# The state-space stage of a two-layer trunk: three spreads, both own products, the output weights and the PE's overflow loops moved

## The reference

```python
u   = rms_norm(x).reshape(b, s, 64 groups, 16)
bu  = einsum('blgc,gpc->blgp', u, bbar)            # complex, 64 states a group
x_k = scan of  x_k = abar * x_{k-1} + bu_k  over the 256 positions
y   = Re(C x_k) + d_skip * u
y   = gelu(y);  a, g = split(y @ w_out);  out = a * sigmoid(g)
```

## Time and profile before

| | us |
|---|---|
| median of three runs | 727.4 |
| lowest, highest | 727.02, 729.13 |
| the profiled execution, in all | 729.73 |
| its span, first to last instruction | 728.0 |
| PE busy in the span | 633.8 |
| DVE, ACT, POOL busy | 192.7, 136.9, 190.2 |
| mean granted TensorE clock | 0.949 |
| DMA, mean over the span | 335 GB/s |

### The profile page before, as it was taken

One profiled execution on the slowest core, in us unless ns is written; L12 is line 12 of the kernel. 1 busy time (PEld: TensorE's weight loads), 2 busy tenths in 40 slices (PEclk: granted clock), 3 DMA queues, 4 the chain that ended last, 5 costly groups with the idle time before them and its releaser, 6 DMA issues.

```text
span 728.0 us, 13207 instructions
## 1 busy us (share of the span) xinstructions
PE 633.8 (87%) x5575; PEld 404.7 (56%) x5575; DVE 192.7 (26%) x499; ACT 136.9 (19%) x301; POOL 190.2 (26%) x226
## 2 busy tenths in 40 slices
PE   8999998999999988999496989999999699596473
PEld 6888886777556646666162655446564366253130
DVE  3234233255231023102012780126302013002003
ACT  3111322232021011020014331004211012010003
POOL 1001120250699997781941000021000000000001
PEclk9999999999998999799799899999999899899898
DMA  9997967555999999999999556965798999999992
GB/s 313 352 296 158 379 172 228 217 198 215 406 421 420 423 419 415 406 425 420 423 381 344 183 160 265 422 273 203 292 423 346 424 421 422 419 421 421 420 396 75
DMA packets 86707, 244.21 MB, mean 335 GB/s; under 512 B 28052, under 2 KB 56948, under 8 KB 62580
## 3 DMA queue, kind: packets, MB, share of 16 engines
q1 hardware_dynamic: 85188, 237.50, 84.7%
q0 software_dynamic: 1056, 5.24, 1.9%
q10 hardware_dynamic: 400, 0.57, 0.3%
HBM read 239.08 MB, written 4.22 MB: 334 GB/s over the span
## 4 chain that ended last, share of the span: by engine, by line
PE 70%; DMA 20%; SPq 3%; issue 2%; DVE 2%; ACT 2%; POOL 0%; DVEq 0%; POOLq 0%
DMA ring<-in_moe_w_down 11%; PE ps L1962 11%; DMA ring<-in_moe_w_up 9%; PE ps L1698 8%; PE ps L2238 8%; PE ps L2002 7%; PE ps L1833 6%; PE ps L2022 4%; PE ps L1701 4%; PE ps L1762 4%; PE ps L1678 3%; PE ps L1829 2%; SPq L467 2%; PE ps L1895 1%; PE ps L1800 1%
## 5 line engine op out<-in xcount | busy, mean ns | idle before, releaser
L1962 PE MATMUL ps<-ring,xg 128*32 128x256 f32 x1904 | 126.3, 405 | 29.2 <-DMA ring<-in_moe_w_gate 15.1
L1962 PEld LDWEIGHTS ps<-ring,xg 128*32 128x32 f32 x1904 | 70.7, 117 | 80.1 <-issue 51.9
L2002 PE MATMUL ps<-ring,hidT 128*32 128x512 f32 x488 | 65.2, 655 | 18.1 <-DMA ring<-in_moe_w_down 14.0
L2022 PE MATMUL ps<-y_sb,pickT 128*128 128x512 f32 x128 | 59.5, 605 | 3.1 <-ACT y_sb L1012 1.6
L1698 PE MATMUL ps<-xnT,ring 128*128 128x256 f32 x256 | 57.8, 382 | 1.1 <-ACT xnT L888 0.8
L845 POOL TENSOR_TENSOR xh<-x,normw 128x1024 f32<-128x1024 f32 x1 | 2.4, 2357 | 213.3 <-DVE x L1413 213.3
L2238 PE MATMUL ps<-ring,yT 128*128 128x512 f32 x128 | 56.3, 595 | 1.6 <-ACT yT L1065 0.9
L1698 PEld LDWEIGHTS ps<-xnT,ring 128*128 128x128 f32 x256 | 47.8, 190 | 9.0 <-issue 1.0
L1418 DVE TENSOR_TENSOR hid<-sg,ps 128x256 f32<-128x256 f32 (+1 forms) x18 | 7.2, 399 | 163.4 <-ACT sg L985 152.2
L2002 PEld LDWEIGHTS ps<-ring,hidT 128*32 128x32 f32 x488 | 16.6, 119 | 51.5 <-issue 44.9
L1833 PE MATMUL ps<-pick,xn 128*128 128x256 f32 x192 | 44.0, 382 | 0.0
(11 more groups left out here) (370 smaller groups left out, 861.2 us busy)
## 6 DMA issues: line engine op xcount, KB each, us to landing
ring<-in_moe_w_up SPq DMA_DIRECT2D x59, 1024.0 KB, 17.3
ring<-in_moe_w_gate SPq DMA_DIRECT2D x59, 1024.0 KB, 12.7
ring<-in_moe_w_down SPq DMA_DIRECT2D x53, 1024.0 KB, 16.8
ring<-in_attn_w_qkv SPq DMA_DIRECT2D x11, 1024.0 KB, 11.8
ring<-in_moe_w_down SPq DMA_DIRECT2D x16, 512.0 KB, 13.2
ring<-in_ssm_w_out SPq DMA_DIRECT2D x8, 1024.0 KB, 12.4
ring<-in_attn_w_o SPq DMA_DIRECT2D x4, 1024.0 KB, 10.5
chunk_inputs<-turned POOLq DMA_DIRECT2D x3, 1024.0 KB, 10.5
```

The costliest lines, as they stand in the source:

```text
L1962: ins = mm(ps[CAP * h:CAP * (h + 1), GUB, F * half:F * (half + 1)], p.xg[:, c, CAP * (ROUND * r + h):CAP * (ROUND * r + h + 1)], w, start= ...
L2002: ins = mm(ps[CAP * h:CAP * (h + 1), DNB + b, :], hidT[:, r, j, CAP * h:CAP * (h + 1)], w, start=(j == 0), stop=(j == FT - 1), tile_positi ...
L2022: ins = mm(ps[:, u, :], p.pickT[rows, r, tt * P:(tt + 1) * P], y_sb[rows, r, 512 * b:512 * (b + 1)], start=(r == 0), stop=(r == p.rounds - 1))
```

## The change

Four things change.

1. The spreads 0, 1 and 2 go ahead of the turned rows on PE, and ACT copies them out ahead of three `copy_down`s. The other five stay where they were. To have free banks, the stage's banks get new numbers (`BANK`). PE waits for these three copies ahead of the products with the input map. The filler after regrouping is one matmul instead of two.
2. `own_chunk(1)` follows `own_chunk(0)` directly, ahead of `earlier_chunks(0)`; the three filler matmuls there and the wait on `z_used` are gone.
3. `load_wout(0)` and `(1)` come after the wait for `in_done` 4, and `load_wout(2)` and `(3)` after that for `y_done` 2.
4. PE's loops over further windows stand at the end of its program, and the code that skips them follows the branch directly; the branch hint is gone.

The diff, without the replacements of a bank's number by `BANK[...]`:

```diff
+BANK = (0, 4, 5, 7, 1, 2, 3, 6)
+EARLY_SPREAD = 3
-WARM = {"start": 2, "choice": (5, 3), "ranks": 1, "regrouping": 2, "recurrence": 3, "last lags": 4}
+WARM = {"start": 2, "choice": (5, 3), "ranks": 1, "regrouping": 1, "last lags": 4}
...
+            sp.wait_ge(in_done, 4)
             load_wout(0)
             load_wout(1)
-            sp.wait_ge(in_done, 4)
+            sp.wait_ge(y_done, 2)
             load_wout(2)
             load_wout(3)
-            sp.wait_ge(y_done, 2)
...
             norm_root(2)
+            def take_spread(some):
+                for i in some:
+                    act.wait_ge(toe_done, i + 1)
+                    nc.scalar.copy(toe(SPREAD[i // 2])[:, 512 * (i % 2):512 * (i % 2 + 1)], ps[:, BANK[4 + i % 4], :]).then_inc(u_evac_a, 1)
+            take_spread(range(EARLY_SPREAD))
             for l in (7, 3, 1):
                 copy_down(l)
...
-            take_spread()
+            take_spread(range(EARLY_SPREAD, NT))
...
-            def spread():
-                for i in range(NT):
+            def spread(some):
+                for i in some:
                     l = SPREAD[i // 2]
-                    if i >= 4:
-                        pe.wait_ge(u_evac_a, TOE_COPIES + i - 3)
+                    if i == 4 + EARLY_SPREAD:
+                        pe.wait_ge(u_evac_a, TOE_COPIES + EARLY_SPREAD + 1)
...
-                    if not after:
-                        ahead_of_branch = pe.mark_branch_hint_location()
...
-                windows, passed_by = f"pe_windows_{layer}", f"pe_passed_by_{layer}"
-                pe.br_cmp(most, CAP, on_true=windows, on_false=passed_by, comp_op="IS_GT").branch_hint(ahead_of_branch)
-                with nc.body(windows, valid_engines=[pe.engine]):
+                branch_at[layer] = nc.cur_bb
+                pe.br_cmp(most, CAP, on_true=f"pe_windows_{layer}", on_false=f"pe_passed_by_{layer}", comp_op="IS_GT")
+                nc.switch_bb(f"pe_passed_by_{layer}")
+                pe.nop()
+
+            def windows(layer):
+                with nc.body(f"pe_windows_{layer}", valid_engines=[pe.engine], parent=branch_at[layer]):
...
             regroup((2, 3), regrouped)
-            keep_warm(2, WARM["regrouping"])
+            spread(range(EARLY_SPREAD))
+            keep_warm(6, WARM["regrouping"])
...
             pe.wait_ge(wb_loaded, 32)
+            pe.wait_ge(u_evac_a, TOE_COPIES // 2 + EARLY_SPREAD)
...
-            spread()
+            spread(range(EARLY_SPREAD, NT))
...
             own_chunk(0)
-            pe.wait_ge(z_used, 1)
-            keep_warm(0, WARM["recurrence"])
+            own_chunk(1)
             earlier_chunks(0)
-            own_chunk(1)
             turn_outputs(0)
...
             layer_moe(1)
+            pe.br("pe_end")
+            for layer in range(2):
+                windows(layer)
+            nc.switch_bb("pe_end")
+            pe.nop()
```

More of the change, by code:

```diff
@@ L1062, in take_outputs @@
                     act.wait_ge(yT_turned, 2 * h + b + 1)
-                    src = ps[:, 4 + 2 * h + b, :].rearrange("p (r u b k) -> p r u b k", r=2, u=TT, b=BLK)
+                    src = ps[:, BANK[4 + 2 * h + b], :].rearrange("p (r u b k) -> p r u b k", r=2, u=TT, b=BLK)
                     for r in range(2):
@@ L1083, in _ @@
             norm_root(2)
+            def take_spread(some):
[3 more added lines that the diff above has]
+            take_spread(range(EARLY_SPREAD))
             for l in (7, 3, 1):
                 copy_down(l)
-            def take_spread():
-                for i in range(NT):
-                    act.wait_ge(toe_done, i + 1)
-                    nc.scalar.copy(toe(SPREAD[i // 2])[:, 512 * (i % 2):512 * (i % 2 + 1)], ps[:, 4 + i % 4, :]).then_inc(u_evac_a, 1)
             for h in range(2):
                 act.wait_ge(in_done, 2 * h + 1)
-                nc.scalar.copy(s_in[:, 4 * h:4 * h + 2].rearrange("p j r a s -> p (j r a s)"), ps[:, 4 + 2 * h, :])\
+                nc.scalar.copy(s_in[:, 4 * h:4 * h + 2].rearrange("p j r a s -> p (j r a s)"), ps[:, BANK[4 + 2 * h], :])\
                   .then_inc(in_evac_a, 1)
-            take_spread()
+            take_spread(range(EARLY_SPREAD, NT))
             def gate(i):
@@ L1101, in gate @@
                     act.wait_ge(mix_added, 2 * RING + i - 1)
-                nc.scalar.activation(sig[:, i % 2, :], ps[:, i, WCOL:2 * WCOL], ACT.Sigmoid).then_inc(sig_done, 1)
+                nc.scalar.activation(sig[:, i % 2, :], ps[:, BANK[i], WCOL:2 * WCOL], ACT.Sigmoid).then_inc(sig_done, 1)
             for h in range(2):
@@ L1585, in _ @@
                 dve.wait_ge(in_done, 2 * h + 2)
-                V.tensor_copy(s_in[:, 4 * h + 2:4 * h + 4].rearrange("p j r a s -> p (j r a s)"), ps[:, 5 + 2 * h, :])\
+                V.tensor_copy(s_in[:, 4 * h + 2:4 * h + 4].rearrange("p j r a s -> p (j r a s)"), ps[:, BANK[5 + 2 * h], :])\
                  .then_inc(in_evac_d, 1)
@@ L1598, in recur @@
                     dve.wait_ge(xk_ready, 2 * h)
-                sre, sim = ps[:, 2 * h, :], ps[:, 2 * h + 1, :]
+                sre, sim = ps[:, BANK[2 * h], :], ps[:, BANK[2 * h + 1], :]
                 V.tensor_tensor(zr, sre, co, ALU.mult)
@@ L1632, in glu @@
                 xs = x[:, tt, s * WCOL:(s + 1) * WCOL]
-                lk(V.tensor_tensor(sig[:, i % 2, :], sig[:, i % 2, :], ps[:, i, 0:WCOL], ALU.mult))
+                lk(V.tensor_tensor(sig[:, i % 2, :], sig[:, i % 2, :], ps[:, BANK[i], 0:WCOL], ALU.mult))
                 V.tensor_tensor(xs, xs, sig[:, i % 2, :], ALU.add).then_inc(mix_added, 1)
@@ L1909, in regroup @@
                         ins.then_inc(done, 1)
-            def spread():
-                for i in range(NT):
+            def spread(some):
+                for i in some:
                     l = SPREAD[i // 2]
-                    if i >= 4:
-                        pe.wait_ge(u_evac_a, TOE_COPIES + i - 3)
-                    mm(ps[:, 4 + i % 4, :], ident_pad[:, GC * l:GC * l + P],
+                    if i == 4 + EARLY_SPREAD:
+                        pe.wait_ge(u_evac_a, TOE_COPIES + EARLY_SPREAD + 1)
+                    mm(ps[:, BANK[4 + i % 4], :], ident_pad[:, GC * l:GC * l + P],
                        lags[:, 512 * (i % 2):512 * (i % 2 + 1)], start=True, stop=True).then_inc(toe_done, 1)
@@ L2115, in moe_pe @@
                 combine(p.rounds - 1, (1, 3) if p.closes(p.rounds - 1) else range(4))
+            branch_at = {}
             def layer_moe(layer):
@@ L2146, in layer_moe @@
                         regroup((0, 1))
-                    pe.br(passed_by)
-                nc.switch_bb(passed_by)
-                pe.nop()
+                    pe.br(f"pe_passed_by_{layer}")
             layer_moe(0)
@@ L2191, in _ @@
                     for r in range(2):
-                        ins = nc.tensor.transpose(ps[:, 2 * h + r, cols(jp)], s_in[:, jp, r].rearrange("p a s -> p (a s)"), ident)
+                        ins = nc.tensor.transpose(ps[:, BANK[2 * h + r], cols(jp)], s_in[:, jp, r].rearrange("p a s -> p (a s)"), ident)
                 ins.then_inc(in_turned, 1)
-            spread()
+            spread(range(EARLY_SPREAD, NT))
             def own_chunk(h):
@@ L2214, in earlier_chunks @@
                                 rows = slice(NS * par_g, NS * (par_g + 1))
-                                ins = mm(ps[32 * b:32 * (b + 1), 4 + 2 * h + par_g, cols(i)], xk[rows, r, jp, b, :],
+                                ins = mm(ps[32 * b:32 * (b + 1), BANK[4 + 2 * h + par_g], cols(i)], xk[rows, r, jp, b, :],
                                          wC[rows, 1:LAGS, r, st, :], start=False, stop=(r == 1 and i == JP // 2 - 1),
@@ L2224, in turn_outputs @@
                         pe.wait_ge(gelu_done, 2 * (h + 1))
-                    ins = nc.tensor.transpose(ps[:, 4 + 2 * h + l // 4, cols(l)], y2[:, h, l].rearrange("p j c -> p (j c)"), ident)
+                    ins = nc.tensor.transpose(ps[:, BANK[4 + 2 * h + l // 4], cols(l)], y2[:, h, l].rearrange("p j c -> p (j c)"), ident)
                     if l % 4 == 3:
@@ L2237, in unit @@
                 for kt in range(h, KT, 2):
-                    ins = mm(ps[:, i, :], yT[:, kt, tt * P:(tt + 1) * P], w[:, kt, :],
+                    ins = mm(ps[:, BANK[i], :], yT[:, kt, tt * P:(tt + 1) * P], w[:, kt, :],
                              start=(first and kt == h), stop=(last and kt == KT - 2 + h))
```

10 lines of the change are left out of this document (5 added, 5 removed).

## The result

The changed kernel took 723.48 us as the median of 10 runs (721.34 to 725.81), the kernel before 729.01 over 10 runs (725.64 to 730.52). The ratio is 0.993, with a 95% interval of 0.9915 to 0.9946: 5.1 us faster (3.9 to 6.2), where 9.1 was forecast; 723.48 lies above the range that ended at 723.0. Of the 5.2 between it and the forecast median of 718.3, 1.6 are not the change's: the prediction started from 727.4 for the kernel before, which took 729.01 here. The gain doesn't depend on this, and it is little more than half of the forecast one. The sign and most steps were right. Two steps were not: the supply of instructions, and the arrival of slot 2's output weights.

What follows compares the result with a forecast made beforehand. PE ahead of its first expert pass was taken as the bound, with the DMA-bound tail hanging on it. Terms -3.73 - 0.94 + 0.29 - 2.58 - 0.82 - 1.68 + 0.4 = -9.06 took 727.4 to 718.3 us; range 716.2 to 723.0.

Steps and rivals of the forecast that it cites:

- a: PE's branch ahead of regrouping: nothing fetched out of order, regrouping starts at 396.20 instead of 399.93, -3.73 us.
- b: Regrouping on PE: its 32 records run at full clock, 1.08 us instead of 2.02, -0.94.
- R1: Rival: the fetch at PE's branch stays; 719.2 us if it lasts 3.77, 724.2 if 6.53; chance 0.06.
- c: After regrouping: three spreads and one filler replace two fillers, 3.44 us for 3.15, +0.29; ACT's early copies cost nothing.
- e: Own products: both in a row without filler, -0.82 us; `y_done` 1 at 420.41 instead of 428.20.
- f: After `y_done` 1: PE waits for gelu alone, 1.20 us instead of 2.88, -1.68; first output unit at 423.58.
- i: Instruction supply over own products and state outputs, 512 small PE instructions: taken as 0, bounds 0 and 1.8 us.
- g: Late output weights: slots 0 and 1 cost nothing, slot 2 costs +0.4 us at unit (4,0), bounds 0 and 8.
- h: Rest of SP's queue: still stretch begins at 498.5 instead of 505, should end at 503; 4.5 us of cover left.
- R2: Rival: the tail does not follow, layer 1's late loads fill the still stretch; 725.8 us at 12 too good; chance 0.05.
- R3: Rival, slower: slot 2's late weights hold the output product at unit (4,0); 729.5 us if they take 20; chance 0.04.
- R4: Rival: PE's clock falls once more in gaps near 403, 421 and 423, costing 2 to 3 us; 720.3 to 721.3; chance 0.12.

Runs made afterwards that it cites:

- slots 0 and 1 early: Changed kernel with output weights of slots 0 and 1 loaded as early as before, slots 2 and 3 still behind `y_done` 2; 722.72 us, ratio 0.9914.
- changed, shifted: Changed kernel with 32 tiny matmuls (128 PE instructions) added at the start, shifting where PE's instruction blocks end; 744.8 us, one run.
- old branch: Changed kernel with the loop body again between PE's branch and its target, with the hint; ratio to the kernel before 1.0022.
- all weights early: Changed kernel with all output weights issued as before the change; ratio to the kernel before 0.9913.
- own products alone: Kernel before with only both own products put together, no filler and no wait on `z_used`; ratio 1.0022.
- both with shifted blocks: Changed kernel, and the same with output weights spread over the stage, each with 32 tiny matmuls added at the start; 744.8 and 738.4 us, one run each.
- the no-ops: Changed kernel with 128 no-ops at the start of PE's program; 723.57 us, a single run.

## Why the prediction was wrong, step by step

**a, b, the branch and the clock: right.** 3.81 and 0.87 against 3.73 and 0.94. The 0.12 for the signal was my estimate; in the trace after it was 0.05. The 0.94 stood on the clock staying up: PE's gap ahead of regrouping shrank from 4.58 to 0.78, and the granted clock over it was 1.00. The untaken branch lasted 0.09. R1 fell. Its sum for 6.53 was a little off: in the kernel before the granted clock was 0.50 from 397.6 to 404.4, so of its four matmuls half the clock reached only the first two, which took 3.15, and not nearly three; with two more at 0.86 that is 4.9, not 4.7.

**c, d, the spreads: right.** The fillers and spreads took 3.63 for 3.44, the five spreads 4.31 for 4.30. ACT's three early copies hid: PE waited for none of them.

**e, f, the own products and gelu: right but for i.** From the start of the own products to `y_done` 1 were 8.39, where 5.86 was forecast. In the kernel without the stall (slots 0 and 1 early) it was 5.71, so the whole difference is the stall's. Gelu to the first unit was 3.20, forecast 3.17.

**i, the supply of instructions: the step that failed.** I put it at 0, with 1.8 as its bound. The stall was 2.33, and the first unit came 2.68 later than in the kernel without it. The bound was an estimate of mine: 3.77, the price of a fetch at an idle moment (a DMA share of 0.02 over that branch), less the 1.96 in which 256 records run, about as many as one packet stands for. But the prediction itself had just explained 6.53 by a fetch that lay beside 4 MB of output weights, and part 3 moves such a load into the very stretch in which the 512 short instructions run. With the 2.76 between those two the bound would have been 4.6; the longest stalls were 3.22 (changed, shifted) and 3.33 (old branch). These matmuls are small, with weights 32 columns wide: 128 of them with their 128 loads are run in 2.0 (L2224) to 3.7 (L2211), and ten of the thirteen kernels stall in this stage, for 0.5 to 3.3. Of the seventeen jumps that PE took over its loops, fourteen lasted 3.4 to 6.5.

**g, slot 2's weights: mis-sized.** The wait was named at the right place, unit (4,0), but was 2.4, not 0.4. The stall made `y_done` 2 late, and the request with it, so that alone would have changed nothing; the pair took 10.2 after `y_done` 2, where I had taken 8.4 from one earlier pair. From the start of unit (2,0) to that of (4,0) it was 7.85 in every kernel that didn't wait, and 8.6 to 10.4 in the six that load slot 2 there and had to. The row was one draw of a spread, and it stood as the value with 8 as the upper bound of the wait. Why the same pair takes 8.4 one time and 10.2 another stays open.

**The sum again:** from unit (2,0) to (4,0) took 10.38 instead of 7.85, 2.53, where the sum had 0.4. 9.06 less 2.68 and less 2.1 is 4.3; the stage showed 4.07, and the other 0.2 is small differences such as the first rows of the table show. The ratio says 5.1 (3.9 to 6.2).

**h and R2, the tail: right.** The DMA share was 0.01 from 497 to 504; the still stretch was forecast from 498.5 to 503. Layer 1's loads didn't fill it. **R3** and **R4** named real things, a late slot 2 and a falling clock; the wait was 2.4, where R3 was priced with 11.6. (A pair that takes 20 makes PE wait 20 - 8.0 = 12.0, so R3's sum should have been +2.5, not +2.1; nothing else hangs on it.) The granted clock held through the mixer in the changed kernel (1.00 from 368.6 to 491.5), but fell to 0.50 there in five of the variants. Each of these had a fetch stall. With the old branch it fell in the stall, with all weights early right behind it, in the other three (own products alone, and both with shifted blocks) in the gaps of PE around gelu that follow. Stalls of 2.3 and 2.5, in the changed kernel and in that with the no-ops, went without a fall, and no run shows what decides it.

**The range** was too narrow on the side of the unknowns. Its end lay 4.7 above the forecast, about enough for 1.8 at i and 3 at g, but not for the bound of 8 that g had been given, nor for the 4.6 that i should have had. The two terms cost 4.8 together, beyond the 0.4 that the sum had for g. On the 729.01 of the kernel before in these runs, the same range would have ended at 724.6 and taken 723.48 in; with that luck the two steps would have been as wrong.

## What to carry to other kernels

When a stretch of short PE instructions is moved or packed, price its instruction fetch with the DMA traffic that will lie beside it, and look at where your own edit puts that traffic. A load that is moved "later, since it isn't needed yet" can still collide with something: moved from early to late, slots 0 and 1 met the block's packet, and the stall was 2.33 instead of 0. Of the four orders tried here the best was neither early nor late but spread, the last two slots behind one event each, which turned a gain of 5.1 into 9.5. Late weights had helped only by clearing the way for the fetch at the branch. Once another edit has removed such a cause, the edit that eased its symptom should be tried again without.

## What the runs showed of the hardware

- A jump of PE with an instruction packet moved in it: 3.4 to 3.8 in the twelve that had idle DMA engines (shares of 0.01 to 0.04), 6.1 and 6.5 in the two that had them full of the 1 KB packets of the output weights (1.07 and 1.09). An untaken branch: 0.06 to 0.09. The difference lies ahead of the packet, which starts 0.9 to 1.5 after the jump begins with idle engines and 3.5 and 3.9 after it with full ones; from there it is 2.3 to 2.9 in both.
- With the hint, the jump at layer 0 lasted 3.6 to 6.5 in four kernels. The same branch at layer 1 lasted 0.36, 0.36 and 0.45 in three of them, and 3.77 in the kernel before. What decides this, and whether the hint has a part in it, was not tried.
- One late block of PE instructions: 0 (three kernels) to 1.0 where the output weights were over, 0.8 (two kernels) where they had just ended, 0.5 to 3.3 where the block's packet moved among them. Its place moved by 64 matmuls when 128 matmul and weight-load instructions were added 400 us earlier; 128 no-ops moved nothing (2.45 behind the same record).
- 32 matmuls of 16 columns at the start of the program took 13.8 us, 0.43 each. The two of 512 columns behind them took 3.76, 1.88 each, where one takes 0.86 in the stage at a granted clock of 1.00. So 0.43 is a price of that place in the program; what sets it no run shows.
